# Second norm of a transformer-like step: broadcast ahead of three modulation units, a weight split on GpSimd

## The chip, the cores and the metric

One core of one Trainium2 chip. The metric is the device time of one execution in microseconds, median over runs. The engines are TensorE (PE: matmuls, PEld: its weight loads), VectorE (DVE), ScalarE (ACT), GpSimd (POOL) and SyncE (SP, which issues most DMAs).

## The reference

Two layers over 128 context tokens and 512 latent tokens, D = 1024, all float32. What matters here is the second norm and the MLP behind it, and the modulation vectors:

```python
m = (jax.nn.silu(cvec) @ w_mod[l] + b_mod[l])[..., None, :]
sh1, sc1, g1, sh2, sc2, g2 = jnp.split(m, N_MOD, axis=-1)
...
x = x + g1 * (jnp.concatenate([o, y], axis=-1) @ w_out[l])
h2 = _rmsnorm(x, norm2_g[l]) * (1 + sc2) + sh2
a, b = jnp.split(_dwconv3(h2 @ w_up[l], ffn_conv_w[l]), 2, axis=-1)
x = x + g2 * ((jax.nn.silu(a) * b) @ w_down[l])
```

## The kernel before, in words

Activations lie transposed: features on the 128 partitions, eight tiles k of them, and T = 644 columns for all tokens (both sequences with zero columns between), in two halves of 322. Each float32 product is made of three matmuls on rounded parts: a value v is split into hi = round(v) and lo = v - hi, and hi*hi, hi*lo and lo*hi are summed in PSUM.

Weights come in units of 128x2048 into two slots of `raw`, n = 0 to 17 in each layer; unit n uses slot n % 2. SP loads a unit, ACT makes `w_hi` (`split_hi`, L1238), DVE makes `w_lo` = raw - w_hi (`split_lo`, L1675), and PE uses both and frees the slot (`unit_done`). The order on every engine is written out by hand, and semaphores tie the engines together. Units 12 to 15 are the output projection. Units 16 (`G_U`) and 17 (`G_U + 1`) are w_up columns of the two "plain" gates, 0 and 6, computed directly; the other 20 gates go through a Strassen-like scheme of seven products, for which SP loads blocks (L518) and GpSimd issues DMAs that add one block to another (L621).

Around the second norm ("the gap") the program has this order:

- PE: the output projection's last chain; `mod_turn` (four 128x128 transposes of `mod_row`, L714); `stat` (one-column matmuls that sum x squared, L726); two modulation units on `mod_t` (`mod_sum`, L703, 8 small matmuls each; the trace counts every float32 matmul twice); `spread` (ones times a diagonal matrix, which puts 1/rms of every token on all partitions, L735); two modulation units on `mod_x`; `mod_turn`; then gate 0 in eight tiles k (`gate_tile`, L1049 to L1051), each after `h2_ready`, with another `mod_turn` behind tile 4; then gate 1, which waits for `split_full[1]`.
- ACT: `square` of each tile of x (L1393); the square root (`rms`, L1227); `rows`, a copy of the modulation sums out of PSUM (L1193), which waits for both `mod_t` units; `split_hi` of unit 17; then for each tile `h_full` (gain and shift, two instructions, L1411) and `h_high` (rounding to `hc_hi`, L1419), with another `rows` behind tile 2.
- DVE: the last addition to x; `reciprocals` (1/rms and the five 128x128 diagonals, L1666), which needs the square root; then for i = 0 to 9 the multiplication of x by the broadcast (L1976, for tile i) and the subtraction that gives `hc_lo` (L1984, for tile i - 2, after `h_high`). `mod_post` (L1621, L1624: adds the modulation parts) stands in turn i = 2 and `split_lo` of unit 17 in turn i = 5. After the loop the transformed inputs of the Strassen-like scheme are made.
- POOL: two loads and two stores early in the layer, then block sums only. SP: its first w_up block waits for `split_full[1]` of unit 17.

The modulation units of the gap are `GAP_A[l]` and the next: 10 and 11 in layer 0, 6 and 7 in layer 1. None of them is used by the second norm of its own layer.

Of the kernel before, what the change touches and what calls it, by code (L numbers as in the profile page):

```python
# [7 lines left out]
F32 = mybir.dt.float32  # L8
# [196 lines left out]
def hybrid_step(nc, x_prompt, x_sample, cache_k, cache_v, c_sample, c_ctx, w_mod, b_mod, norm1_g, w_in, q_norm_g,  # L205
# [3 lines left out]
    with ctx:  # L209
# [389 lines left out]
        @block.gpsimd  # L599
        def _(pool):  # L600
            ck = cache_k.rearrange("b l p h s d -> p (b l) (h s d)")
            cv = cache_v.rearrange("b l p h e -> p (b l) (h e)")
            nk = new_k.rearrange("b l p h s d -> p (b l) (h s d)")
            nv = new_v.rearrange("b l p h e -> p (b l) (h e)")
            for l in range(DEPTH):
                if l:
                    pool.wait_ge(stat_full, 3 * l + 1)
                else:
                    pool.wait_ge(rms_ready, 1)
                    pool.wait_ge(xT_read, 2 + KT)  # L610
                pool.dma_start(kc[:, :], ck[:, ds(l, 1), :].rearrange("p a n -> p (a n)")).then_inc(kv_in, 16)
                pool.wait_ge(mod_used, MOD_LAYER * l + MOD_PRE + 4)
                pool.dma_start(v[:, 1, :], cv[:, ds(l, 1), :].rearrange("p a n -> p (a n)")).then_inc(v_in, 16)
                pool.wait_ge(qk_ready, 2 * NT * l + NT + 1)
                pool.dma_start(nk[:, ds(l, 1), :].rearrange("p a n -> p (a n)"), qn[:, 0, :]).then_inc(nk_out, 16)
                pool.wait_ge(v_ready, NT * l + 1)
                pool.dma_start(nv[:, ds(l, 1), :].rearrange("p a n -> p (a n)"), v[:, 0, :]).then_inc(out_done, 16)

                def add_block(dst, src, which):

                    pool.dma_start(raw_f[:, BLK * dst:BLK * (dst + 1)], raw_f[:, BLK * src:BLK * (src + 1)],  # L621
                                   accum_op=ALU.add).then_inc(sum_full[which], 16)

                def first_sum(g):

                    a22, b = a22_block(g), s1_block(g)
                    pool.wait_ge(blk_full[a22], loaded(l, g, a22))
                    pool.wait_ge(blk_full[b], loaded(l, g, b))
                    add_block(b, a22, 1)

                first_sum(FIRST)
                for g in S_GATES:
                    pool.wait_ge(sum_full[1], summed(l, g))
                    pool.wait_ge(blk_full[2], loaded(l, g, 2))
                    add_block(2, s1_block(g), 2)
                    pool.wait_ge(blk_full[0], loaded(l, g, 0))
                    pool.wait_ge(blk_full[4], loaded(l, g, 4))
                    add_block(4, 0, 4)
                    pool.wait_ge(sum_full[2], summed(l, g))
                    pool.wait_ge(blk_full[5], loaded(l, g, 5))  # L640
                    add_block(5, 2, 5)
                    if g != S_GATES[-1]:
                        first_sum(S_GATES[S_GATES.index(g) + 1])
            pool.wait_ge(out_done, 16 * DEPTH)
            pool.wait_ge(nk_out, 16 * DEPTH)
# [17 lines left out]
        def _(pe):  # L663
# [12 lines left out]
            def mod_sum(l, h, u, b, landed_at):  # L676

                if b == "x" or b == "t":
                    pe.wait_ge(modx_full if b == "x" else modt_full, 32 * (l + 1))
                    wu = (mod_x if b == "x" else mod_t)[:, u, :].rearrange("p (t n) -> p t n", n=UC)  # L680
                    if b == "t" and u == 0:
                        pe.wait_ge(mod_ready, MOD_LAYER_G * l + h + MOD_PRE_G)
                elif b == "q":
                    pe.wait_ge(modq_full[2 * h + u], 16 * (l + 1))
                    wu = mod_q[:, 2 * h + u, :].rearrange("p (t n) -> p t n", n=UC)
                    if u == 0:
                        pe.wait_ge(mod_ready, MOD_LAYER_G * l + h + MOD_PRE_G)
                elif l is None:
                    if h == 1 and u == 0:
                        pe.wait_ge(mod_ready, 1)  # L690
                    elif h == 3 and u == 0:
                        pe.wait_ge(mod_ready, 3)
                    pe.wait_ge(pre_full[2 * h + u], 32)
                    wu = pre_unit(2 * h + u).rearrange("p (t n) -> p t n", n=UC)
                else:
                    pe.wait_ge(raw_full[b], landed_at)
                    wu = raw[:, b, :].rearrange("p (t n) -> p t n", n=UC)
                    if u == 0:
                        pe.wait_ge(mod_ready, MOD_LAYER_G * l + h + MOD_PRE_G)
                for part in range(2):  # L700
                    for q in range(4):
                        k = 4 * part + q
                        ins = mm(ps[QUAD * q:QUAD * (q + 1), mod_bank(l, h), u * UC:(u + 1) * UC], cT[:, k, :],  # L703
                                 wu[:, k, :], start=part == 0, stop=part == 1)
                ins.then_inc(mod_used, 1)
# [24 lines left out]
            def spread(l, which):  # L730

                for t, off, n, h, p0 in TILE_CUTS:
                    if off == 0:
                        pe.wait_ge(diag_ready, 3 * NT * l + (NT * which + t + 1))
                    ins = mm(ps[:, B_RMS[which][h], p0:p0 + n], ones[:, :], diag[:, t * P + off:t * P + off + n],  # L735
                             start=True, stop=True)
                    if off + n == P:
                        ins.then_inc(rb_full, 1)
# [47 lines left out]
            for l in range(DEPTH):  # L786
# [245 lines left out]
                    mod_turn(l, 9)  # L1032
                stat(l, 2)

                for u in range(2):
                    mod_sum(l, GAP_A[l], u, "t", None)
                spread(l, 2)
                for u in range(2):
                    mod_sum(l, GAP_A[l] + 1, u, "x", None)
                mod_turn(l, GAP_A[l])  # L1040
# [139 lines left out]
        def _(act):  # L1180
            A = nc.scalar.activation

            def rows(l, h):


                if l is None:
                    n = PRE_ORDER.index(h)
                    act.wait_ge(mod_used, 2 * n + 2)
                    if n:
                        act.wait_ge(modT_full, n)  # L1190
                else:
                    act.wait_ge(mod_used, MOD_LAYER * l + (MOD_PRE + 2 * h + 2))
                A(mod_row[:, :], ps[:, mod_bank(l, h), :], ACT.Copy).then_inc(row_read, 1)  # L1193
# [49 lines left out]
            for l in range(DEPTH):  # L1243
                def split_hi(n, i=None, size=SLOT):
                    split_hi_of(l, n, i, size)

                def rms(which, scale):
                    rms_of(l, which, scale)
# [147 lines left out]
                for n in range(4):  # L1396
                    square(2 * n)
                    if l < LAST:
                        rows(l, 6 + n)
                    square(2 * n + 1)  # L1400
                    if n < 3:
                        split_hi(O_U + n + 2)
                rms(2, 1.0 / D)
                rows(l, GAP_A[l])
                split_hi(G_U + 1)

                def h_full(k):

# [6 lines left out]
                def h_high(k):  # L1415

                    act.wait_ge(hf_ready, KT * l + k + 1)
                    base = k // KH * T
                    A(hb_hi[:, k % KH, base:base + T], hfull[:, k, :], ACT.Copy).then_inc(hh2_ready, 1)  # L1419

                h_full(0)
                h_high(0)
                h_full(1)
                for k in range(1, KT):
                    if k < KT - 1:
# [180 lines left out]
        def _(dve):  # L1606
# [91 lines left out]
            for l in range(DEPTH):  # L1698
# [275 lines left out]
                for i in range(KT + 2):  # L1974
                    if i < KT:
                        V.tensor_tensor(hfv[:, i, :, :], x[:, i, :].rearrange("p (h n) -> p h n", h=2),  # L1976
                                        ps[:, b0:b1 + 1, 0:HALF], ALU.mult).then_inc(xr_ready, 1)
                    if i == 2:
                        mod_post(l, GAP_A[l])
                    if i >= 2:  # L1980
                        k = i - 2
                        base = k // KH * T
                        dve.wait_ge(hh2_ready, KT * l + k + 1)
                        V.tensor_tensor(hb_lo[:, k % KH, base:base + T], hfull[:, k, :],  # L1984
                                        hb_hi[:, k % KH, base:base + T].bitcast(F32), ALU.subtract
                                        ).then_inc(h2_ready, 1)
                    if i == 5:
                        split_lo(G_U + 1)
                mod_post(l, GAP_A[l] + 1)

                h11, h12, h21, h22 = (hfv[:, KH * i:KH * (i + 1), h, :] for i in range(2) for h in range(2))
# [216 lines left out]
```

## Time and profile before

| | us |
|---|---|
| median of 3 runs | 1636.96 (1635.1 to 1638.65) |
| profiled execution, device time | 1639.15 |
| its span, first to last instruction | 1637.3 |
| PE busy in it | 1568.9 |
| DVE, ACT, POOL busy | 1032.3, 726.0, 142.7 |

In the timelines a row has the start in us from the span's start, the duration, engine, line, operation, what is written and read, the shapes, how many instructions the row merges and, in brackets, how long the engine stood idle before it and what released it. A row with xN covers N instructions from the first's start to the last's end.

### The profile page before, as it was taken

What the parts mean: (1) busy time and instruction counts of PE and PEld (TensorE: products, weight loads), DVE (VectorE), ACT (ScalarE), POOL (GpSimd) and SP (SyncE); (2) the same over time, 40 slices, a digit from 0 to 9 for tenths busy, and PEclk for the clock granted to TensorE, in tenths of its full rate; (3) what the DMA queues carried; (4) which work ended last, traced back from release to release, by engine and by line L of the source; (5) the groups of instructions that cost most, each with busy time, mean ns of one, the idle gap of its engine ahead of it and who ended that gap; (6) DMA issues with size and microseconds to landing.
All of it is one profiled execution on the core that took longest, in us unless ns stands there. A gap on an engine that the chain in (4) does not pass through costs nothing. (4 is left out here: it accounts for less than half of the span.)

```text
span 1637.3 us, 26294 instructions
## 1 busy us (share of the span) xinstructions
PE 1568.9 (96%) x10543; PEld 1460.5 (89%) x10543; DVE 1032.3 (63%) x1654; ACT 726.0 (44%) x1214; POOL 142.7 (9%) x172
## 2 busy tenths in 40 slices
PE   6999999988999999999979999999999999999998
PEld 4677888977999999999976788889899999999998
DVE  5752666645775765757776527667488667476573
ACT  3533444325662543525443344443366345163451
POOL 0000000000211201212000000000012011120210
PEclk9999999999999999999979999999999999999999
DMA  9555010473775956759631540115169476594862
GB/s 355 173 180 168 27 52 30 135 234 104 172 177 136 203 151 158 177 157 209 209 101 61 182 138 27 51 35 164 36 159 213 136 178 159 137 224 129 190 162 81
DMA packets 284043, 236.13 MB, mean 144 GB/s; under 512 B 10448, under 2 KB 254736, under 8 KB 283920
## 3 DMA queue, kind: packets, MB, share of 16 engines
q1 hardware_dynamic: 259392, 189.82, 37.0%
q0 software_dynamic: 23680, 44.05, 15.8%
q8 instruction: 84, 1.38, 0.4%
q10 hardware_dynamic: 848, 0.56, 0.1%
q14 instruction: 39, 0.32, 0.1%
HBM read 188.78 MB, written 3.67 MB: 118 GB/s over the span
## 5 line engine op out<-in xcount | busy, mean ns | idle before, releaser
L621 POOL DMA_DIRECT2D raw_all<-raw_all x160 | 137.9, 879 | 1130.5 <-DMA raw_all<-in_w_up_dram 996.1
L1512 ACT ACTIVATE w_hi<-raw_all 128x1024 fp32r<-128x1024 f32 x120 | 126.2, 1056 | 236.6 <-DMA raw_all<-raw_all 114.0
L1130 PE MATMUL ps<-gg,w_hi 128*128 128x322 f32 x704 | 219.2, 311 | 0.0
L1132 PE MATMUL ps<-gg,w_lo 128*128 128x322 f32 x704 | 218.7, 311 | 0.0
L2042 DVE TENSOR_TENSOR w_lo<-raw_all,w_hi 128x1024 fp32r<-128x1024 f32 x120 | 146.7, 1222 | 114.0 <-ACT w_hi L1512 113.3
L1131 PE MATMUL ps<-gg,w_hi 128*128 128x322 f32 x704 | 218.4, 310 | 0.0
L1075 PE MATMUL ps<-hc_lo,w_hi 128*128 128x322 f32 x640 | 199.6, 312 | 0.0
L1077 PE MATMUL ps<-hc_hi,w_lo 128*128 128x322 f32 x640 | 198.9, 311 | 0.0
L1073 PE MATMUL ps<-hc_hi,w_hi 128*128 128x322 f32 x640 | 198.7, 310 | 0.0
L1073 PE MATMUL ps<-ht_hi,w_hi 128*128 128x322 f32 x480 | 151.2, 315 | 5.7 <-ACT s L1530 3.6
L1077 PE MATMUL ps<-ht_hi,w_lo 128*128 128x322 f32 x480 | 149.0, 310 | 0.0
L1075 PE MATMUL ps<-ht_lo,w_hi 128*128 128x322 f32 x480 | 148.9, 310 | 0.0
L2003 DVE SCALAR_TENSOR_TENSOR tmp<-ub,vecs,tmp 128x642 f32<-128x642 f32 x168 | 139.5, 883 | 13.5 <-ACT tmp L1470 13.4
L1938 DVE SCALAR_TENSOR_TENSOR x<-ps,modv,x 128x128 f32<-128x128 f32 (+2 forms) x240 | 90.4, 434 | 90.6 <-PE ps L1132 53.7
L1675 DVE TENSOR_TENSOR w_lo<-raw_all,w_hi 128x2048 fp32r<-128x2048 f32 x36 | 82.4, 2289 | 95.3 <-ACT w_hi L1238 95.2
L1132 PEld LDWEIGHTS ps<-gg,w_lo 128*128 128x128 f32 x704 | 132.9, 189 | 0.0
L1131 PEld LDWEIGHTS ps<-gg,w_hi 128*128 128x128 f32 x704 | 132.8, 189 | 0.0
L1130 PEld LDWEIGHTS ps<-gg,w_hi 128*128 128x128 f32 x704 | 132.5, 188 | 0.1
L671 PE MATMUL ps<-h_hi,w_hi 128*128 128x322 f32 x384 | 122.7, 320 | 0.0
L1073 PEld LDWEIGHTS ps<-hc_hi,w_hi 128*128 128x128 f32 x640 | 120.8, 189 | 0.0
L1077 PEld LDWEIGHTS ps<-hc_hi,w_lo 128*128 128x128 f32 x640 | 120.6, 188 | 0.0
L1075 PEld LDWEIGHTS ps<-hc_lo,w_hi 128*128 128x128 f32 x640 | 120.4, 188 | 0.0
(206 smaller groups left out, 3455.8 us busy)
## 6 DMA issues: line engine op xcount, KB each, us to landing
raw_all<-in_w_up_dram SPq DMA_DIRECT2D x280, 256.0 KB, 3.8
raw_all<-raw_all POOLq DMA_DIRECT2D x160, 256.0 KB, 4.0
raw_all<-in_w_in_dram SPq DMA_DIRECT2D x48, 512.0 KB, 4.6
raw_all<-in_w_mod_dram SPq DMA_DIRECT2D x48, 512.0 KB, 4.4
raw_all<-in_w_down_dram SPq DMA_DIRECT2D x16, 768.0 KB, 4.4
raw_all<-in_w_down_dram SPq DMA_DIRECT2D x16, 640.0 KB, 4.2
mod_q<-in_w_mod_dram SPq DMA_DIRECT2D x8, 1024.0 KB, 11.2
raw_all<-in_w_out_dram SPq DMA_DIRECT2D x16, 512.0 KB, 4.4
```

The source lines that it names most:

```text
L621: pool.dma_start(raw_f[:, BLK * dst:BLK * (dst + 1)], raw_f[:, BLK * src:BLK * (src + 1)], accum_op=ALU.add).then_inc(sum_full[which], 16)
L671: mm(out, wh[:, k, col:col + P], mov_hi(k), start=k == 0, stop=False)
L1073: mm(out, whi_f[:, c0:c0 + P], hh[:, k, slot, :], start=first and k == 0, stop=False, skip_group_check=not first)
L1075: mm(out, whi_f[:, c0:c0 + P], hl[:, k, slot, :], start=False, stop=False, skip_group_check=not first)
L1077: ins = mm(out, wlo_f[:, c0:c0 + P], hh[:, k, slot, :], start=False, stop=k == KH - 1, skip_group_check=not first)
L1130: mm(out, wh[:, k, :], gh, start=k == 0, stop=False)
L1131: mm(out, wh[:, k, :], gl, start=False, stop=False)
L1132: ins = mm(out, wl[:, k, :], gh, start=False, stop=k == kf - 1)
L1512: A(whi_b[:, 2 * i:2 * (i + 1), :], src, ACT.Copy).then_inc(up_hi[i], 1)
L1938: ins = V.scalar_tensor_tensor(out=xs, in0=ps[:, banks[h], p0:p0 + n], scalar=gate, in1=xs, op0=ALU.mult, op1=ALU.add)
L2003: return V.scalar_tensor_tensor(out=cen[:, s, 1:T - 1], in0=u[:, s, j:j + T - 2], scalar=vecs[:, l, w:w + 1], in1=cen[:, s, 1:T - 1], op0= ...
L2042: V.tensor_tensor(wlo_b[:, pair, :], raw_b[:, pair, :] if i else first_pair(g), whi_b[:, pair, :].bitcast(F32), ALU.subtract).then_inc(up_ ...
```

## The change

Four edits, in both layers. PE: the second `mod_t` unit comes after `spread`. ACT: `split_hi` of unit 17 comes right behind the last square, ahead of `rms`; the first `rows` comes behind `h_high(0)`. DVE: the first `mod_post` stands in turn i = 3, and `split_lo` of unit 17 is gone. POOL: it makes that low half, with a `tensor_tensor` of its own that waits for `hi_done[1]` and signals `split_full[1]`.

```diff
--- before.py
+++ after.py
@@ -628,6 +628,9 @@
                     pool.wait_ge(blk_full[b], loaded(l, g, b))
                     add_block(b, a22, 1)
 
+                pool.wait_ge(hi_done[1], l * SPLIT_SLOT + (G_U + 1) // 2 + 1)
+                nc.gpsimd.tensor_tensor(w_lo[:, 1, :], raw[:, 1, :], w_hi[:, 1, :].bitcast(F32), ALU.subtract
+                                        ).then_inc(split_full[1], 1)
                 first_sum(FIRST)
                 for g in S_GATES:
                     pool.wait_ge(sum_full[1], summed(l, g))
@@ -1032,9 +1035,9 @@
                     mod_turn(l, 9)
                 stat(l, 2)
 
-                for u in range(2):
-                    mod_sum(l, GAP_A[l], u, "t", None)
+                mod_sum(l, GAP_A[l], 0, "t", None)
                 spread(l, 2)
+                mod_sum(l, GAP_A[l], 1, "t", None)
                 for u in range(2):
                     mod_sum(l, GAP_A[l] + 1, u, "x", None)
                 mod_turn(l, GAP_A[l])
@@ -1400,9 +1403,8 @@
                     square(2 * n + 1)
                     if n < 3:
                         split_hi(O_U + n + 2)
+                split_hi(G_U + 1)
                 rms(2, 1.0 / D)
-                rows(l, GAP_A[l])
-                split_hi(G_U + 1)
 
                 def h_full(k):
 
@@ -1420,6 +1422,7 @@
 
                 h_full(0)
                 h_high(0)
+                rows(l, GAP_A[l])
                 h_full(1)
                 for k in range(1, KT):
                     if k < KT - 1:
@@ -1975,7 +1978,7 @@
                     if i < KT:
                         V.tensor_tensor(hfv[:, i, :, :], x[:, i, :].rearrange("p (h n) -> p h n", h=2),
                                         ps[:, b0:b1 + 1, 0:HALF], ALU.mult).then_inc(xr_ready, 1)
-                    if i == 2:
+                    if i == 3:
                         mod_post(l, GAP_A[l])
                     if i >= 2:
                         k = i - 2
@@ -1984,8 +1987,6 @@
                         V.tensor_tensor(hb_lo[:, k % KH, base:base + T], hfull[:, k, :],
                                         hb_hi[:, k % KH, base:base + T].bitcast(F32), ALU.subtract
                                         ).then_inc(h2_ready, 1)
-                    if i == 5:
-                        split_lo(G_U + 1)
                 mod_post(l, GAP_A[l] + 1)
 
                 h11, h12, h21, h22 = (hfv[:, KH * i:KH * (i + 1), h, :] for i in range(2) for h in range(2))
```

PE in layer 0, from the last transposes of the output projection to gate 0. Before:

```order
L726 MATMUL ps<-ones,sq 128x1 x5
L703 MATMUL ps<-mod_t,cT 32x256 x16
L735 MATMUL ps<-sq,ones 128x128 x2
L735 MATMUL ps<-sq,ones 128x64 x2
L735 MATMUL ps<-sq,ones 128x128 x2
L703 MATMUL ps<-mod_x,cT 32x256 x16
L714 MATMUL ps<-ident,mod_row 128x128 x4
L1049 MATMUL ps<-hc_hi,w_hi 128x322
```

With the change:

```order
L729 MATMUL ps<-ones,sq 128x1 x5
L706 MATMUL ps<-mod_t,cT 32x256 x8
L738 MATMUL ps<-sq,ones 128x128 x2
L738 MATMUL ps<-sq,ones 128x64 x2
L738 MATMUL ps<-sq,ones 128x128 x2
L706 MATMUL ps<-mod_t,cT 32x256 x8
L706 MATMUL ps<-mod_x,cT 32x256 x16
L717 MATMUL ps<-ident,mod_row 128x128 x4
L1052 MATMUL ps<-hc_hi,w_hi 128x322
```

Eight of the sixteen `mod_t` matmuls moved behind the six of `spread`.

ACT in layer 0, from the last square on (`w_hi` is unit 17's high half, `mod_row` the row copy, `hfull` the shift). Before:

```order
L1393 ACTIVATE sq<-x 128x644
L1227 ACTIVATE rms<-rms,eps 128x5
L1193 ACTIVATE mod_row<-ps 128x512
L1238 ACTIVATE w_hi<-raw_all 128x2048
L1411 ACTIVATE hfull<-hfull,modv,gain 128x128
L1411 ACTIVATE hfull<-hfull,modv,gain 128x512
L1419 ACTIVATE hc_hi<-hfull 128x644
L1411 ACTIVATE hfull<-hfull,modv,gain 128x128
L1411 ACTIVATE hfull<-hfull,modv,gain 128x512
L1411 ACTIVATE hfull<-hfull,modv,gain 128x128
```

With the change:

```order
L1396 ACTIVATE sq<-x 128x644
L1241 ACTIVATE w_hi<-raw_all 128x2048
L1230 ACTIVATE rms<-rms,eps 128x5
L1413 ACTIVATE hfull<-hfull,modv,gain 128x128
L1413 ACTIVATE hfull<-hfull,modv,gain 128x512
L1421 ACTIVATE hc_hi<-hfull 128x644
L1196 ACTIVATE mod_row<-ps 128x512
L1413 ACTIVATE hfull<-hfull,modv,gain 128x128
L1413 ACTIVATE hfull<-hfull,modv,gain 128x512
L1413 ACTIVATE hfull<-hfull,modv,gain 128x128
```

The high half moved ahead of the square root, and the row copy behind the first tile's `hc_hi`.

DVE in layer 0, from turn i = 4 of the loop on (`w_lo` is unit 17's low half). Before:

```order
L1976 TENSOR_TENSOR hfull<-x,ps 128x644
L1984 TENSOR_TENSOR hc_lo<-hfull,hc_hi 128x644
L1976 TENSOR_TENSOR hfull<-x,ps 128x644
L1984 TENSOR_TENSOR hc_lo<-hfull,hc_hi 128x644
L1675 TENSOR_TENSOR w_lo<-raw_all,w_hi 128x2048
L1976 TENSOR_TENSOR hfull<-x,ps 128x644
L1984 TENSOR_TENSOR hc_lo<-hfull,hc_hi 128x644
L1976 TENSOR_TENSOR hfull<-x,ps 128x644
L1984 TENSOR_TENSOR hc_lo<-hfull,hc_hi 128x644 x3
```

With the change, and below it GpSimd's queue where the work went:

```order
L1979 TENSOR_TENSOR hfull<-x,ps 128x644
L1987 TENSOR_TENSOR hc_lo<-hfull,hc_hi 128x644
L1979 TENSOR_TENSOR hfull<-x,ps 128x644
L1987 TENSOR_TENSOR hc_lo<-hfull,hc_hi 128x644
L1979 TENSOR_TENSOR hfull<-x,ps 128x644
L1987 TENSOR_TENSOR hc_lo<-hfull,hc_hi 128x644
L1979 TENSOR_TENSOR hfull<-x,ps 128x644
L1987 TENSOR_TENSOR hc_lo<-hfull,hc_hi 128x644 x3
```

```order
L615 DMA out_dram<-qn 128x512
L617 DMA out_dram<-v 128x512
L632 ISA
L632 TENSOR_TENSOR w_lo<-raw_all,w_hi 128x2048
L621 DMA raw_all<-raw_all 128x512 x80
```

The subtraction of 128x2048 left DVE and stands on GpSimd between the layer's last store and its first block sum, with an ISA instruction ahead of it in layer 0 (none in layer 1).

## Rows read from the trace of the kernel before

**Rows 1.** First part of the page: busy us, share, instructions of each engine.
```profile
PE 1568.9 (96%) x10543; PEld 1460.5 (89%) x10543; DVE 1032.3 (63%) x1654; ACT 726.0 (44%) x1214; POOL 142.7 (9%) x172
```
**Rows 2.** Waits of PE over the span: total us, times, longest.
```profile
PE ps L1049 <- DVE hc_lo L1984: 7.5, 6, 1.6
```
**Rows 3.** Timeline of PE in layer 1's gap.
```profile
1175.51 1.93 PE L703 MATMUL ps<-mod_t,cT 128*32 128x256 f32 x32
1177.38 1.60 PE L735 MATMUL ps<-sq,ones 128*128 128x128 f32 x12
...
1182.86 0.39 PE L1049 MATMUL ps<-hc_hi,w_hi 128*128 128x322 f32 x1 [1.43 <-DVE hc_lo L1984]
...
1189.50 0.42 PE L1049 MATMUL ps<-hc_hi,w_hi 128*128 128x322 f32 x1
...
1193.18 0.41 PE L1049 MATMUL ps<-hc_hi,w_hi 128*128 128x322 f32 x1 [1.63 <-DVE hc_lo L1984]
```
**Rows 4.** Timeline of ACT in layer 1's gap.
```profile
1173.51 0.74 ACT L1393 ACTIVATE sq<-x 128x644 f32<-128x644 f32 x1 [6.38 <-DVE x L1938]
1175.82 0.30 ACT L1227 ACTIVATE rms<-rms,eps 128x5 f32<-128x5 f32 x1 [1.57 <-DVE rms L1660]
1177.51 0.60 ACT L1193 ACTIVATE mod_row<-ps 128x512 f32<-128x512 f32 x1 [1.39 <-PE ps L703]
1178.01 1.90 ACT L1238 ACTIVATE w_hi<-raw_all 128x2048 fp32r<-128x2048 f32 x1
...
1181.76 2.28 ACT L1411 ACTIVATE hfull<-hfull,modv,gain 128x128 f32<-128x128 f32 x4
1183.94 0.72 ACT L1419 ACTIVATE hc_hi<-hfull 128x644 fp32r<-128x644 f32 x1
...
1185.66 0.72 ACT L1419 ACTIVATE hc_hi<-hfull 128x644 fp32r<-128x644 f32 x1
...
1187.86 0.72 ACT L1419 ACTIVATE hc_hi<-hfull 128x644 fp32r<-128x644 f32 x1
...
1192.42 1.20 ACT L1411 ACTIVATE hfull<-hfull,modv,gain 128x128 f32<-128x128 f32 x2 [2.11 <-DVE hfull L1976]
```
**Rows 5.** Timeline of DVE in layer 1's gap and after it.
```profile
1176.42 1.07 DVE L1666 TENSOR_SCALAR sq<-ident,rms 128x128 f32<-128x128 f32 x5
1179.02 2.29 DVE L1976 TENSOR_TENSOR hfull<-x,ps 128x644 f32<-128x644 f32 x3 [1.52 <-PE ps L735]
...
1184.69 0.83 DVE L1984 TENSOR_TENSOR hc_lo<-hfull,hc_hi 128x644 fp32r<-128x644 f32 x1 [1.25 <-ACT hc_hi L1419]
...
1189.37 2.28 DVE L1675 TENSOR_TENSOR w_lo<-raw_all,w_hi 128x2048 fp32r<-128x2048 f32 x1
...
1217.65 1.22 DVE L2042 TENSOR_TENSOR w_lo<-raw_all,w_hi 128x1024 fp32r<-128x1024 f32 x1 [3.89 <-ACT w_hi L1512]
```
**Rows 6.** Stretches: us, then busy us of PE, PEld, DVE, ACT, POOL; PEclk; DMA.
```profile
380.00:384.00 4.00, 4.00 (x35) 1.81 (x35) 1.44 (x7) 0.66 (x2) 0.00 (x0) 0.50 0.00 0
1200.90:1215.40 14.50, 14.50 (x99) 14.50 (x98) 12.64 (x11) 7.20 (x9) 4.32 (x5) 1.00 0.74 165
```
**Rows 7.** Timeline of PE, ACT and DVE in layer 0's gap.
```profile
378.02 1.99 PE L726 MATMUL ps<-ones,sq 128*128 128x1 f32 x10 [0.55 <-ACT sq L1393]
379.94 3.64 PE L703 MATMUL ps<-mod_t,cT 128*32 128x256 f32 x32
380.25 0.30 ACT L1227 ACTIVATE rms<-rms,eps 128x5 f32<-128x5 f32 x1 [2.28 <-DVE rms L1660]
383.50 2.41 PE L735 MATMUL ps<-sq,ones 128*128 128x128 f32 x12
385.96 2.30 DVE L1976 TENSOR_TENSOR hfull<-x,ps 128x644 f32<-128x644 f32 x3 [4.04 <-PE ps L735]
388.70 2.28 ACT L1411 ACTIVATE hfull<-hfull,modv,gain 128x128 f32<-128x128 f32 x4
```
**Rows 8.** Groups by line of POOL: busy us, mean ns of one.
```profile
L2196 POOL MEMSET const-float32-0.0<- 128x1 f32 x1 | 0.1, 98 | 0.2 <-issue 0.2
```
**Rows 9.** Timeline of SP's DMA queue in layer 1's gap.
```profile
1191.68 38.61 SPq L518 DMA_DIRECT2D raw_all<-in_w_up_dram  x20
```

## The prediction

> **What bounds the kernel now.** I read the profile's first part, then the waits of the tensor engine (PE), then the timelines of PE, ScalarE (ACT) and VectorE (DVE) through the gap between output projection and first plain gate, in both layers, and last the clock and the DMA queue there. PE is busy 96% of the span and ends last [rows 1]: an edit pays only if it shortens PE's own idle time or its slow stretches. One of PE's largest waits is the first plain gate waiting for hc_lo, 7.5 us in 6 waits over two layers [rows 2]. The change works just there.
>
> The timeline of layer 1 shows the gap at full clock [rows 3]: two mod_t units run from 1175.51 for 1.93 us, then the broadcast (`spread`, L735) for 1.60, then two mod_x units and the transposes, and gate 0 starts at 1182.86. But DVE had begun the diagonals for the broadcast at 1176.42 and finished at 1177.49 [rows 5]: the second mod_t unit kept it waiting. After that the work is a chain for each of 8 tiles k: DVE multiplies x by the broadcast (0.82 us), ACT shifts it (two instructions, 1.2 us) and rounds it to hc_hi (0.74), DVE subtracts to hc_lo (0.83), PE computes tile k of gate 0. Starts overlap the previous instruction's end by some 0.1 us, so ACT needs 1.72 us per tile (1183.94 to 1185.66), and 2.2 us where it also copies a row of modulation (1185.66 to 1187.86) [rows 4]. PE needs 1.8 us per tile, since gate 1, eight like tiles, takes 14.5 us unbroken [rows 6]. ACT and PE are thus nearly level, and any delay in the chain reaches PE. One is large: DVE's 2.28 us split_lo at 1189.37 makes ACT wait 2.11 us for its next tile, and PE 1.63 us before tile 4 [rows 3, 4, 5].
>
> Layer 0 has the same gap with one difference: the granted clock stands at 0.50, the 1.2 GHz level, over 380 to 384. The mod_t units take 3.64 us instead of 1.93, the broadcast 2.41 instead of 1.60 [rows 3, 6, 7].
>
> **The broadcast earlier.** In layer 1 the first mod_t unit, half of 1.93, ends at 1176.5. ACT now makes the high half right behind the last square: it starts as the square ends, about 1174.2, and lasts 1.90, to 1176.1, so the rms square root, at 1175.82 before, slips by 0.2 us [rows 4], and the diagonals end at 1177.7. The broadcast follows them one by one, and its last tile lands about 0.5 us behind the last diagonal, at 1178.2, where before it ended at 1178.98. DVE's first multiply starts **0.8 us earlier**. In layer 0 the square root waits for the statistics anyway (380.25); the square there ends at about 377.9, as PE's matmuls on it start at 378.02, so the high half is done at about 379.8, in time; first unit 379.94 to 381.8, broadcast 2.4 at the low clock, to 384.25: DVE starts **1.7 us earlier** than 385.96 [rows 7].
>
> **The row copy behind the first tile.** `rows`, 0.6 us, stood with the high half before the first shift, both hidden by the wait for the broadcast. It now stands between h_high(0) and h_full(1), on the chain, and costs its 0.5 to 0.6 there. So h_full(1) moves by 0.8 - 0.5 = 0.3 us in layer 1 (1181.76 to 1181.45) and by 1.7 - 0.5, about 1.25, in layer 0 (388.70 to 387.45) [rows 4, 7]. The transposes wait for this copy: PE stands idle about 0.6 us in front of them, and gate 0 starts at 1182.0, 0.85 earlier, but tile 1 only 0.3 earlier. The moved modulation sum on DVE (0.36 us) falls into a wait of 1.25 for hc_hi and costs nothing. The modulation unit moved past the broadcast costs nothing: the same instructions, needed by nothing before the row copy.
>
> **split_lo off DVE.** ACT's wait of 2.11 us vanishes. Late next is PE itself: tile 3 starts at 1189.50, so tile 4 could at 1191.3 and starts at 1193.18 [rows 3]; **1.9 us per layer** go. Nothing takes its place, since the remaining chain goes at 1.72 us against PE's 1.8.
>
> **The subtraction on GpSimd.** No trace row shows GpSimd doing arithmetic on a tile. From below the nearest row is DVE's same instruction, 2.28 us [rows 5]; GpSimd's own nearest is a 128x1 memset of 98 ns [rows 8], a fixed cost only. From above I can bound it only by its cover: gate 1 needs it at 404.6 in layer 0 and 1198.6 in layer 1 (new times), and the high half is ready at 379.8 and 1176.1. Anything up to 22.5 us costs nothing; I take it so, because the row on DVE is ten times shorter than that cover. The GPSIMD Engine Reference of the Trainium skill (Performance versus the Vector engine) gives 4.5 us for a 2048-element fp32 tensor_tensor, twice VectorE's; the sum would be the same by it. Behind this wait on GpSimd's queue stands only the first block sum of the layer, whose blocks are loaded after the subtraction in any case. The DMA queue waits for the same semaphore before its w_up blocks: it starts them some 10 us earlier than 1191.68 [rows 9], with nothing else to move; no gain, as ACT's first up-split also needs gate 0's end.
>
> **The sum.** Layer 1: 1.9 + 0.3 = 2.2. Layer 0: 1.9 + 1.25 = 3.15. Together 5.3 us off a span of 1637.3, leaving 1632.0. Behind gate 0 stand 14.5 us of gate 1, in which DVE runs out of work and then idles 3.89 us for the next high half [rows 5], and its work has moved forward as far as PE's; later phases are PE's, so the gain is kept. The profiled execution took 1639.15, 2.2 above the median of 1636.96, and the clock step of layer 0 may be missing in other runs: then layer 0 gains what layer 1 does. I forecast 1636.96 - 5.2 = **1631.8 us**. A measurement of this kernel tells about 0.2%, 3.3 us, from no change, so faster means below 1633.7.
>
> **Rivals.**
> *Port.* DVE runs slower beside GpSimd. At stake are the instructions between high half and end of the subtraction: diagonals 1.07 and three multiplies 2.29 [rows 5]. If they all took twice as long: 3.4 us a layer at worst, 6.7 in all, and the gain is gone; half of that, a size between nothing and the worst, gives about 1635. Against it: two of the three ends are guesses, and in layer 0 the multiplies start 4.4 us after the high half. The GPSIMD Engine Reference (Key points) says that GpSimd shares its SBUF interfaces with VectorE and collides with instructions in a 2-port mode or with two SBUF inputs. By that rule the multiplies, with one input in PSUM, would be spared. No row of this trace can decide it.
> *Clock.* The low level seen at 380 to 384 came right after sparse one-column matmuls and a 0.55 us wait [rows 6, 7]. The new order adds a wait before the broadcast and one before the transposes. If layer 1 falls to 0.5 as well, the first mod_t unit takes 0.9 longer and the broadcast 0.8, and with the latency behind it some 2 us are given back: about 1634.
> *GpSimd late.* If its subtraction ends after gate 0, PE waits for it, and the change is slower. It decides from 22.5 us (layer 1) and 24.6 (layer 0); break-even over both is about 26. At 30 us gate 1 would start at 409.8 and 1206.1 instead of 407.7 and 1200.9, 2.1 + 5.2 = 7.3 us later than before: 1644. For it: nothing shows GpSimd's speed, and the new order has an extra ISA instruction ahead of the first subtraction, whose price no row shows. Against it: ten times DVE's time.
> *Nothing carried.* The gaps close but another wait in front of gate 1 or the up phase, such as the transformed inputs on DVE, takes the time: 1637. Against it: gate 1 runs unbroken, and DVE's work ends before it does [rows 5, 6].
>
> **Chances.** Forecast 0.66; port 0.13, clock 0.10, late GpSimd 0.05, nothing carried 0.06. The forecast's own spread is 1629.5 to 1634 (the scatter of runs, 1635.1 to 1638.65, and the clock step present or not); port and clock reach to 1635.5. I give 1629.0 to 1635.6. Faster: nearly all of the forecast and a third of clock, 0.68. Same: the rest of these and nothing carried, 0.25. Slower: late GpSimd and the worst of port, 0.07.
>
> **What would show it.** Right: no PE wait before tile 4; PE's wait for hc_lo at about 3 us instead of 7.5; the broadcast starting within 0.4 us of the first diagonal; the subtraction on GpSimd over before 390 and 1190; the DMA queue's first block there too. Wrong: a wait of PE for GpSimd at gate 1; diagonals or multiplies longer than 0.28 and 0.82; a PE clock under 1.0 in layer 1's gap; PE idle in the first up products.

## The result, and the profile after

The change made the kernel **slower**: 1639.77 us median (20 runs) against 1636.34 for the kernel before (20 runs), ratio 1.0028 with a 95% interval of 1.0019 to 1.0037. (The two medians alone would give 1.0021, which the interval contains.) I had forecast 1631.8 and a range of 1629.0 to 1635.6. The profiled execution has a span of 1640.2 us, 2.9 above the one of before.

Waits of PE in the changed kernel (total us, times, longest):

```profile
PE ps L738 <- DVE sq L1669: 8.2, 3, 4.0
...
PE ps L1052 <- DVE hc_lo L1987: 1.7, 2, 1.1
```

The wait that the change was to shorten did shrink, from 7.5 us [rows 2] to 1.7. A new one of 8.2 us stands in its place: `spread` (now L738) waits for the diagonals (L1669). Timeline of layer 1's gap, PE and POOL, to be held against [rows 3]:

```profile
1175.41 1.28 PE L706 MATMUL ps<-mod_t,cT 128*32 128x256 f32 x16
1180.66 2.93 PE L738 MATMUL ps<-sq,ones 128*128 128x128 f32 x12 [3.98 <-DVE sq L1669]
1183.52 1.94 PE L706 MATMUL ps<-mod_t,cT 128*32 128x256 f32 x16
...
1190.68 0.41 PE L1052 MATMUL ps<-hc_hi,w_hi 128*128 128x322 f32 x1 [0.61 <-DVE hc_lo L1987]
```
```profile
1176.03 4.49 POOL L632 TENSOR_TENSOR w_lo<-raw_all,w_hi 128x2048 fp32r<-128x2048 f32 x1 [224.77 <-ACT w_hi L1241]
```

and DVE in the same stretch, against [rows 5]:

```profile
1176.17 0.19 DVE L1666 RECIPROCAL rms<-rms 128x5 f32<-128x5 f32 x1 [0.49 <-ACT rms L1230]
1176.44 4.95 DVE L1669 TENSOR_SCALAR sq<-ident,rms 128x128 f32<-128x128 f32 x5
1183.63 2.30 DVE L1979 TENSOR_TENSOR hfull<-x,ps 128x644 f32<-128x644 f32 x3 [2.24 <-PE ps L738]
```

The five diagonals take 4.95 us instead of 1.07. The view of that one line (min, median, max of its five instructions, ns) shows how it is shared out:

```profile
L1669 DVE TENSOR_SCALAR sq<-ident,rms x5: 274/274/4169, 1176.4 to 1181.1; 128x128 f32<-128x128 f32 x5
```

One instruction takes 4.17 us, the other four 0.27 each. The long one began at 1176.44 and so ended at about 1180.6; GpSimd's subtraction ended at 1176.03 + 4.49 = 1180.52. DVE did not go slower: it **stood still until GpSimd was done**. PE stood still with it. The granted clock was at the 1.2 GHz level through that wait and the broadcast behind it. The stretch 1174 to 1186 in the kernel before, then in the changed one (columns as in [rows 6]):

```profile
1174.00:1186.00 12.00, 9.58 (x105) 7.12 (x106) 6.94 (x16) 9.01 (x15) 0.00 (x0) 1.00 0.01 2
```
```profile
1174.00:1186.00 12.00, 7.82 (x62) 5.43 (x66) 7.61 (x10) 3.62 (x6) 4.54 (x2) 0.59 0.36 104
```

The mean granted clock there is 0.59 instead of 1.00, and the broadcast takes 2.93 us instead of 1.60. The wait didn't bring the clock down, though. Two short stretches of the changed kernel show the fall while PE was still busy with the first `mod_t` unit, before the wait began at about 1176.7:

```profile
1175.00:1176.00 1.00, 1.00 (x17) 0.81 (x20) 0.17 (x1) 1.00 (x2) 0.00 (x0) 1.00 0.00 0
1176.00:1176.50 0.50, 0.50 (x12) 0.00 (x0) 0.25 (x2) 0.14 (x1) 0.47 (x1) 0.63 0.00 0
```

So two things are mixed here, the hold and the clock. The experiments take them apart.

A measure for all that follows is the **gap length**: from the first `stat` matmul to the first matmul of the first Strassen-like product. Both ends are rows of the PE timeline. Before: 376.30 to 422.05 and 1172.14 to 1215.11, so 45.75 us in layer 0 (low clock in part) and 42.97 in layer 1 (full clock). With the change: 378.22 to 424.10 and 1172.04 to 1218.31, so 45.88 and 46.27. Together 3.4 us more, where the spans differ by 2.9. Outside the gaps the profiled executions scatter by a few us (e7 below has gaps 7.0 us shorter than the kernel before, and a span 12.2 us shorter), so for the gap I go by gap lengths, and for the time of a kernel by the ratios.

### The profile page after: what moved, and what is told of

It is laid out like the page before. It is cut to its first block and busy times, and to the rows that moved or that the text cites. A ratio compares the mean times of both kernels' runs of the same rounds, so it can differ in the third digit from the quotient of the medians.

```text
span 1640.2 us, 26296 instructions
## 1 busy us (share of the span) xinstructions
PE 1571.1 (96%) x10543; PEld 1463.8 (89%) x10543; DVE 1036.7 (63%) x1652; ACT 725.8 (44%) x1214; POOL 150.4 (9%) x174
## 5 line engine op out<-in xcount | busy, mean ns | idle before, releaser
L1678 DVE TENSOR_TENSOR w_lo<-raw_all,w_hi 128x2048 fp32r<-128x2048 f32 x34 | 77.8, 2289 | 96.6 <-ACT w_hi L1241 96.5
```

## The experiments

Ratios are to the kernel before, run on the same chip, five rounds each.

| run | ratio (95%) | gap, layer 0 / 1, us |
|---|---|---|
| the change | 1.0028 (1.0019 to 1.0037) | 45.88 / 46.27 |
| e1 GpSimd behind the diagonals | 0.9977 (0.9961 to 0.9992) | 42.91 / 42.44 |
| e2 low half back on DVE | 1.0009 (0.9998 to 1.0021) | 44.86 / 44.29 |
| e3 before, low half on GpSimd | 1.0012 (1.0001 to 1.0024) | 44.65 / 44.94 |
| e4 diagonals with two inputs | 1.0035 (1.0023 to 1.0047) | 45.95 / 46.35 |
| e5 diagonals on ACT | 0.9994 (0.9981 to 1.0008) | 41.96 / 43.84 |
| e6 e1, old order on PE | 0.9988 (0.9976 to 0.9999) | 40.66 / 42.67 |
| e7 e1 with dense fillers | 0.9961 (0.9947 to 0.9975) | 40.65 / 41.09 |
| e8 GpSimd behind the first hc_hi | 1.0017 (1.0002 to 1.0032) | 44.95 / 43.84 |
| e9 before with dense fillers | 0.9997 (0.9985 to 1.0009) | 43.18 / 43.60 |
| e10 the change with dense fillers | 1.0018 (1.0005 to 1.0031) | 45.88 / 46.28 |
| e11 e1 with sparse fillers | 0.9975 (0.9962 to 0.9987) | 41.93 / 42.28 |
| e12 e5 with dense fillers | 0.9965 (0.9952 to 0.9978) | 40.88 / 42.59 |

### Is it GpSimd, or the new order? (e1, e2)

e1 is the change with one wait more on GpSimd:

```diff
                 pool.wait_ge(hi_done[1], l * SPLIT_SLOT + (G_U + 1) // 2 + 1)
+                pool.wait_ge(diag_ready, 3 * NT * l + 3 * NT)
```

> GpSimd's subtraction waits for the five diagonals as well, all else as in the change. Theory A (only VectorE's tensor_scalar on the SBUF tile, the diagonals, is held by GpSimd's tensor_tensor; multiplies with one operand in PSUM are not): diagonals 1.1 us again, three multiplies 2.3 us, the time comes out where I forecast the change, 5 us below the kernel before (ratio 0.997). Theory B (any VectorE instruction that reads SBUF is held): the three multiplies take 5 to 6 us and hc_lo(0) is late, time 2 to 6 us above the kernel before. Theory C (the new order on TensorE and ScalarE costs, not GpSimd): time stays 3 to 5 us above the kernel before.

Timeline of e1, layer 1, DVE, then POOL:

```profile
1173.10 1.07 DVE L1670 TENSOR_SCALAR sq<-ident,rms 128x128 f32<-128x128 f32 x5
1176.41 2.29 DVE L1980 TENSOR_TENSOR hfull<-x,ps 128x644 f32<-128x644 f32 x3 [2.24 <-PE ps L739]
```
```profile
1174.32 4.56 POOL L633 TENSOR_TENSOR w_lo<-raw_all,w_hi 128x2048 fp32r<-128x2048 f32 x1 [227.92 <-DVE sq L1670]
```

One wait turns 1.0028 into 0.9977. The diagonals are back at 1.07 us, and the three multiplies, one operand of each in PSUM, run inside GpSimd's 4.56 us at 2.29, untouched. Theory A holds, B falls, and C falls as the explanation of the change's time. The gain of 3.7 us is short of the 5 expected. Per layer the hold had cost 45.88 - 42.91 = 3.0 and 46.27 - 42.44 = 3.8 us of gap in these profiles.

e2 removes the subtraction from GpSimd and puts `split_lo(G_U + 1)` back into turn i = 5.

> The change with the low half back on VectorE in turn 5 and nothing on GpSimd: the reordering alone. Theories A and B: by the terms of the prediction 0.3 us in layer 1 and 1.25 in layer 0 are won, 1.5 us below the kernel before, ratio 0.999. Theory C: 3 to 5 us above it.

The PE wait before tile 4 is back, at the size of [rows 3] (timeline of PE, layer 1):

```profile
1189.69 0.41 PE L1049 MATMUL ps<-hc_hi,w_hi 128*128 128x322 f32 x1 [1.63 <-DVE hc_lo L1984]
```

The reordering alone won nothing: 1.0009, where I had expected 0.999 (and where theory C would have had at least 1.002). Against e1, which differs in the place of the low half alone, the gaps are 1.95 and 1.85 us longer: the term of 1.9 us per layer for `split_lo` was right.

### Which instructions are held? (e3, e4, e5, e8)

e3 is the kernel before with only the low half moved, where ACT makes the high half after the row copy, as before.

> The kernel before with one edit: the low half on GpSimd instead of VectorE, where ScalarE makes the high half late (ready about 1179.9 in layer 1). Diagonals are over by then. Theory A: the multiplies are untouched, PE's wait before tile 4 is gone, 1.9 us per layer, 3.8 us below the kernel before (0.9977), unless hc_lo(0), with two SBUF inputs, is held until the subtraction ends near 1184.4: then tile 0 starts 2.5 us late per layer and little is won. Theory B: multiplies 5 us, slower by 2 us or more.

DVE and POOL in layer 1:

```profile
1177.64 2.29 DVE L1979 TENSOR_TENSOR hfull<-x,ps 128x644 f32<-128x644 f32 x3 [3.15 <-PE ps L738]
1180.09 0.19 DVE L1624 TENSOR_REDUCE modv<-ps 128x8 f32<-128x32 f32 x1 [0.15 <-PE ps L717]
1180.35 2.39 DVE L1627 TENSOR_TENSOR modv<-modv,vecs 128x8 f32<-128x8 f32 x1
```
```profile
1178.16 4.55 POOL L632 TENSOR_TENSOR w_lo<-raw_all,w_hi 128x2048 fp32r<-128x2048 f32 x1 [229.80 <-ACT w_hi L1241]
```

The smallest instruction in the loop pays. In the kernel before, this addition of 8 columns, with both inputs in SBUF, was

```profile
1181.74 0.17 DVE L1624 TENSOR_TENSOR modv<-modv,vecs 128x8 f32<-128x8 f32 x1
```

Now it takes 2.39 us and ends at 1182.74, GpSimd at 1182.71. hc_lo(0) queues behind it, so tile 0 is late, though it was not itself the first to be held. That is theory A in a wider form: instructions with two SBUF inputs are held too. The ratio is 1.0012, and not the 0.9977 that I had expected if nothing were held.

e4 writes the diagonals as identity x 1/rms x identity:

```diff
-                    V.tensor_scalar(diag[:, t * P:(t + 1) * P], ident[:, :], rms5[:, t:t + 1], None, ALU.mult
-                                    ).then_inc(diag_ready, 1)
+                    V.scalar_tensor_tensor(out=diag[:, t * P:(t + 1) * P], in0=ident[:, :], scalar=rms5[:, t:t + 1],
+                                           in1=ident[:, :], op0=ALU.mult, op1=ALU.mult).then_inc(diag_ready, 1)
```

> The change with the diagonals made by scalar_tensor_tensor (identity times 1/rms times identity: two SBUF inputs, same values) instead of tensor_scalar, GpSimd early as in the change. If only the one-input tensor_scalar form is held (Theory A, narrow): diagonals about 1.1 us, time 5 us below the kernel before. If two SBUF inputs are held too (A, wide): diagonals near 4.9 us and the time as the change's, 3 to 5 us above. A result between, diagonals of 1.5 to 3 us, would say that the engines share instead of one waiting for the other.

```profile
L1669 DVE SCALAR_TENSOR_TENSOR sq<-ident,rms x5: 338/340/4236, 1176.4 to 1181.3; 128x128 f32<-128x128 f32 x5
```

Held just the same: two SBUF inputs, first instruction 4.24 us. The unheld four also take 0.340 us where tensor_scalar took 0.274. Additions and subtractions with two SBUF inputs take 0.17 us for 8 columns and 0.83 for 644, so about 1.04 ns a column, or 133 ns for 128. An estimate from these rows: 66 ns less for 128 columns is what a tensor_scalar would save that moves its columns at twice the speed. The Trainium skill (Advanced Engine Details and Errata, Mode Summary) says that VectorE moves two elements a cycle in a mode that has source and destination in SBUF and uses two read ports, that the second of these ports is shared with GpSimd, and that the two "will interfere/block eachother". That agrees with the diagonals: 4169 ns against 274.

e5 makes the second norm's diagonals on ACT (copy of the identity with scale 1/rms, behind a semaphore that DVE raises after the reciprocal), GpSimd early as in the change.

> The change with GpSimd as early as in it, but the five diagonals of the second norm made by ScalarE (copy of the identity scaled by 1/rms). If the hold is between GpSimd's tensor_tensor and VectorE's SBUF-only instructions, ScalarE is free of it: diagonals of some 0.25 us each, broadcast not held, multiplies from PSUM 2.3 us as in the first experiment, time near that one (3.8 us below the kernel before), minus half a microsecond per layer for the hand-over. If the SBUF itself were short, ScalarE's diagonals would be long as well (over 3 us) and the time above the kernel before. VectorE's reciprocal (128x5) stands just behind GpSimd's start and may be held: then its start or end slips by up to 4.5 us and this run is as slow as the change.

ACT, DVE and POOL of e5 in layer 1:

```profile
1170.97 1.57 ACT L1411 ACTIVATE sq<-ident,rms 128x128 f32<-128x128 f32 x5 [0.29 <-DVEq L1672]
```
```profile
1170.72 0.19 DVE L1671 RECIPROCAL rms<-rms 128x5 f32<-128x5 f32 x1 [0.37 <-ACT rms L1231]
1174.83 2.29 DVE L1987 TENSOR_TENSOR hfull<-x,ps 128x644 f32<-128x644 f32 x3 [3.92 <-PE ps L739]
```
```profile
1169.68 4.52 POOL L633 TENSOR_TENSOR w_lo<-raw_all,w_hi 128x2048 fp32r<-128x2048 f32 x1 [226.32 <-ACT w_hi L1242]
```

ACT writes the same tile beside GpSimd in 0.3 us apiece: SBUF as such isn't short. The reciprocal, one SBUF input, isn't held either. The ratio, 0.9994, is that of the kernel before, where I had expected some 3 us less. Its interval overlaps e1's; the low clock cost this run too (layer 1, 43.84), and what else it lost I can't say.

e8 lets GpSimd start only after the first `hc_hi` (a wait for `hh2_ready`).

> The change with GpSimd's subtraction waiting for the first hc_hi, so that it runs beside hc_lo(0), multiply 3, the modulation sum and hc_lo(1). If VectorE instructions with all operands in SBUF are held until GpSimd ends (as the modulation sum was at 2.39 us in the third experiment), hc_lo(0) or the next such instruction ends only with GpSimd, TensorE's first tiles start 3 to 4 us late per layer, and the time is 1 to 4 us above the kernel before. If 644-column instructions that have started keep their turn, hc_lo(0) takes 0.83 us and only the next one is held. If two-input ones share, each takes up to twice its time and little is lost.

```profile
1180.13 0.83 DVE L1988 TENSOR_TENSOR hc_lo<-hfull,hc_hi 128x644 fp32r<-128x644 f32 x1 [0.57 <-ACT hc_hi L1422]
1180.88 0.82 DVE L1980 TENSOR_TENSOR hfull<-x,ps 128x644 f32<-128x644 f32 x1
1181.62 0.18 DVE L1625 TENSOR_REDUCE modv<-ps 128x8 f32<-128x32 f32 x1
1181.87 3.54 DVE L1628 TENSOR_TENSOR modv<-modv,vecs 128x8 f32<-128x8 f32 x1
```
```profile
1180.25 5.14 POOL L633 TENSOR_TENSOR w_lo<-raw_all,w_hi 128x2048 fp32r<-128x2048 f32 x1 [231.31 <-ACT hc_hi L1422]
```

Both directions in one picture. hc_lo(0), begun 0.12 us ahead of GpSimd, keeps its 0.83, and GpSimd takes 5.14 instead of 4.5. The next instruction with two SBUF inputs waits 3.5 us, to 1185.41, GpSimd's end being 1185.39; a multiply and a reduction from PSUM between them pass free. **Of two instructions that exclude each other, the one that has begun runs to its end, and the other waits for it**: VectorE's 0.83 us there, GpSimd's 5.14 here.

### And the clock? (e6, e7, e9 to e12)

e6 is e1 with TensorE's order of before, and `rows` again ahead of the first shift.

> The first experiment (GpSimd behind the diagonals, ScalarE's high half early) with TensorE's order of before (both mod_t units ahead of the broadcast) and the row copy hidden in front of the first shift again. By the terms of the prediction: 1.9 us per layer from split_lo, nothing from the broadcast: 3.8 us below the kernel before. If the new TensorE order costs through the clock (it was at 0.50 in all four profiled gaps of the first and second experiments, in one of two in the kernel before), this is as fast as the first experiment or faster, 4 to 6 us below. hc_lo(0), two SBUF inputs, falls beside GpSimd's last half microsecond: if such instructions are held it ends with GpSimd.

Layer 0, at full clock, has a gap of 40.66 us, 2.3 below the full-clock gap of before (layer 1's, 42.97); layer 1 shows 42.67 with its broadcast at 2.64 us. The ratios of e6 and e1 overlap. In layer 1 hc_lo(0) came 1.2 us after GpSimd's end. In layer 0 it began 0.4 us ahead of that end (385.53) and took 1.11 us instead of 0.83:

```profile
385.11 1.11 DVE L1988 TENSOR_TENSOR hc_lo<-hfull,hc_hi 128x644 fp32r<-128x644 f32 x1 [0.57 <-ACT hc_hi L1423]
```

Low clock in these gaps is frequent. In the six profiled gaps with the old TensorE order and no fillers (before, e3, e6) the broadcast took 1.6 us in three and 2.0 to 2.6 in three. In the fourteen with the new order and no dense fillers (change, e1, e2, e4, e5, e8, e11) it took 2.4 to 2.9 in all fourteen. The hold is not the reason, as e1, e2, e5, e8 and e11 have no held diagonals. e7 adds work that is thrown away to e1, in bank 5, which nothing uses there:

```diff
+            def filler(l, n):
+
+                pe.wait_ge(split_full[0], usable(l, G_U))
+                for k in range(n):
+                    mm(ps[:, 5, 0:HALF], w_hi[:, 0, k * P:(k + 1) * P], h_hi[:, k, 0:HALF], start=True, stop=True)
...
+                    if last and which == 2:
+                        filler(l, 4)
...
                 mod_sum(l, GAP_A[l], 0, "t", None)
+                filler(l, 2)
                 spread(l, 2)
```

> The first experiment plus throw-away 128x322 matmuls into an unused PSUM bank, four in TensorE's wait for the last square and two behind the first mod_t unit, per layer. If the low clock in the gap follows from TensorE's own sparse work there, the granted clock stays at 1.00 in both layers more often, the broadcast takes 1.6 instead of 2.9 us, and the time is 2 to 4 us below the first experiment. If the clock falls whatever runs there, the fillers cost their own 0.3 us beside nothing and the time is that of the first experiment or up to 1 us above.

Layer 1 of e7, PE, then DVE, then the stretch from the second `stat` part to the row copy:

```profile
1165.05 1.07 PE L707 MATMUL ps<-mod_t,cT 128*32 128x256 f32 x16
1166.45 1.58 PE L747 MATMUL ps<-sq,ones 128*128 128x128 f32 x12
1167.96 1.07 PE L707 MATMUL ps<-mod_t,cT 128*32 128x256 f32 x16
```
```profile
1168.07 2.29 DVE L1989 TENSOR_TENSOR hfull<-x,ps 128x644 f32<-128x644 f32 x3 [0.92 <-PE ps L747]
1170.93 1.62 DVE L1997 TENSOR_TENSOR hc_lo<-hfull,hc_hi 128x644 fp32r<-128x644 f32 x1 [0.57 <-ACT hc_hi L1431]
```
```profile
1163.80:1170.80 7.00, 6.91 (x88) 4.78 (x88) 3.73 (x10) 3.82 (x5) 3.50 (x1) 1.00 0.01 4
```

Clock 1.00, broadcast 1.58, gaps of 40.65 and 41.09 us, and the lowest ratio of all: **0.9961, 6.3 us below** the kernel before (medians 1630.46 and 1636.77). Its interval overlaps that of e1, so the traces show what the fillers do to the clock, and the times don't yet show a gain from them. hc_lo(0) is held here for 0.8 us, as GpSimd ends at 1171.85.

e9 is the kernel before with the same six fillers, e10 the change with them.

> The kernel before plus the same six throw-away matmuls per layer (four in the wait for the last square, two between the mod_t units): the clock lever without the change. If the gap's clock falls cost the kernel before as well (one of its two profiled gaps stood at 0.50), the clock stays at 1.00 in both and the time is 1 to 3 us below the kernel before, gap of layer 0 near 43 instead of 45.8 us. If the fillers help only the new order, the time is that of the kernel before, plus 0 to 0.6 us for the two fillers that hide behind no wait.

> The change, GpSimd early, plus the same fillers: the hold with the clock kept as far as fillers can. The hold stays, diagonals 4.8 us. The gap should be longer than the 41.1 us of the filler run by the hold, 3.7 us, if the clock survives TensorE's wait of 4 us, and by 5 us or more if it falls in that wait: 45 to 46 us, and 1 to 4 us above the kernel before.

e9 kept the full clock in both gaps (43.18 and 43.60 us) and is no faster: 0.9997, where I had thought 1 to 3 us possible. The fillers don't make a kernel fast by themselves. They also cost something there: e9's layer 1 gap is 0.6 us longer than that of the kernel before (42.97), both at full clock. At full clock the repaired order gives 40.65 and 41.09 against 43.18 and 43.60, so **2.5 us per layer** against e9, and **1.9 us** in layer 1 against the kernel before without fillers.

That gain is not shown to come from the broadcast's new place. e6 has the old order on TensorE and no fillers, and its full-clock layer 0 gap is 40.66, e7's 40.65.

e10 still holds the diagonals (4.96 us). PE in layer 1, then two stretches:

```profile
1170.51 1.07 PE L706 MATMUL ps<-mod_t,cT 128*32 128x256 f32 x16
1171.51 0.56 PE L725 MATMUL ps<-h_hi,w_hi 128*128 128x322 f32 x2
1175.78 2.93 PE L746 MATMUL ps<-sq,ones 128*128 128x128 f32 x12 [3.71 <-DVE sq L1678]
```
```profile
1171.00:1174.50 3.50, 1.07 (x14) 0.39 (x6) 3.15 (x2) 0.24 (x2) 3.37 (x1) 1.00 0.00 0
1175.00:1180.00 5.00, 4.22 (x28) 3.31 (x32) 2.76 (x7) 0.40 (x1) 0.81 (x2) 0.50 0.60 174
```

PE waits 3.71 us, the clock falls in that wait, and the gaps are 45.88 and 46.28: 5.2 us above e7 in each layer. e10 and e7 differ in the one wait on GpSimd alone, and their intervals lie apart. So 5.2 us is the hold's full price where the clock is not already low, the clock lost in PE's wait included.

e11 replaces 322 columns by 16, with 8 and 4 fillers.

> The first experiment with fillers of 16 columns instead of 322, twice as many (8 and 4): TensorE is as unidle as in the filler run but does a tenth of the work. If dense work is what keeps the clock, it falls as in the first experiment: 0.50 in the gap, broadcast 2.9 us, time that of the first experiment (ratio 0.998). If not standing idle is enough, clock 1.00, broadcast 1.6 us, ratio 0.996.

```profile
1169.60:1178.20 8.60, 8.57 (x90) 6.04 (x90) 4.04 (x11) 4.22 (x6) 4.55 (x1) 0.80 0.01 3
```

PE is busy for 8.57 of 8.60 us and the clock still falls (0.80 on average, broadcast 2.71); the ratio is e1's, and its interval overlaps e7's too. So standing idle is not what lowers the clock here. What differs from e7, where it stayed up, is that the fillers are 16 columns wide and not 322, and twice as many. The profiled gaps were 41.93 and 42.28.

> Diagonals on ScalarE, GpSimd early, plus the fillers: no VectorE instruction with SBUF-only operands falls beside GpSimd but possibly none, as GpSimd is over before hc_lo(0). Against the filler run hc_lo(0) is not held (1.62 to 0.83 us), tile 0 starts up to 0.7 us earlier, but the diagonals come about 0.5 us later. Gap 40.5 to 41.5 us per layer, ratio 0.995 to 0.997; a tie with the filler run is the likeliest.

e12 has no held DVE instruction at all, and ties with e7 (0.9965), as expected. Its layer 0 gap, at full clock, is 40.88 where e7 has 40.65; its layer 1 lost the clock in spite of the fillers (broadcast 2.29, gap 42.59). Six fillers are thus no guarantee.

## Why the prediction was wrong, step by step

- **The step that failed is the subtraction on GpSimd, costed at nothing.** I looked for its cover and found 22.5 us, and it was over after 4.5. But I asked only who waits for it, and not whom it makes wait. It runs beside the diagonals, on the critical path, and holds them to its end: 3.0 and 3.8 us per layer (change against e1), 5.2 in each where the clock was up before it (e10 against e7).
- **The rival "port" named the mechanism and missed its size and its victims.** I priced it as instructions taking twice as long, spread over diagonals and multiplies. It is a lock: 0.27 us became 4.17 for one instruction, and the multiplies, which I counted as the larger share, were spared in every run in which they ran beside GpSimd (2.29 or 2.30 us for three in e1, e3, e5, e6, e7, e11 and e12). The rule of the Trainium skill (GPSIMD Engine Reference, Key points) that I cited names two kinds of instruction, those in a 2-port mode and those with two SBUF inputs; I applied it to the multiplies and didn't ask it about the diagonals. With "held until GpSimd ends" the sum was at hand: GpSimd from 1176.1 for its 4.5 us, diagonals done at 1181.6 instead of 1177.7, the gap 3.9 us longer than forecast in layer 1.
- **The rival "clock" also came true**, in every profiled gap of the new order without dense fillers. In layer 1 of e1 it makes the broadcast 1.33 us longer, and the gap is 42.44, where my terms gave 42.97 - 2.2 = 40.8 at full clock. The repaired order won 3.7 us (ratio 0.9977, medians 1633.55 and 1637.25) and not 5.3; the broadcast's 1.33 us are most of the difference, if the profiled gap is typical, which isn't shown.
- **The term of `split_lo` stood**: 1.9 us per layer forecast, 1.95 and 1.85 measured (e2 against e1). PE's wait before tile 4 is gone in the change too; its wait for hc_lo fell to 1.7 us, and I had said about 3. GpSimd's 4.49 us agree with the 4497 ns of the Trainium skill (GPSIMD Engine Reference, Performance versus the Vector engine). SP's first w_up block went from 1191.68 [rows 9] to 1180.55, and no gain from it shows. At full clock the whole repaired order gains 1.9 us in layer 1 (e7 against before) or 2.5 per layer (e7 against e9), against a forecast of 2.2.
- **The term of the broadcast is not confirmed.** The row copy behind tile 0 and the earlier broadcast together were to win 0.3 and 1.25 us. e2 has them alone and is not faster, and e6, without either, has as short a gap at full clock as e7. In layer 0 its gap is 44.86 against 45.75 (0.9 less, both at low clock in part); in layer 1 it is 44.29 against 42.97 at full clock, where it lost the clock.

Two slips in the prediction changed nothing: rounding to hc_hi takes 0.72 us [rows 4] and not 0.74, and the cover in layer 0 is 404.6 - 379.8 = 24.8 us and not 24.6.

What stays open: what the earlier broadcast is worth at full clock; whether fillers pay beyond the noise; and how often each order loses the clock over many runs. The trace shows one execution of each kernel. The mean granted clock over all runs points the same way (0.988 before, 0.983 for the change, 0.986 for e1, 0.989 for e7), but doesn't say where in the span it was lost. Why ScalarE's diagonals in e5 came out no faster than the kernel before is open as well.

## What to carry to other kernels

Before moving elementwise work to GpSimd, list what VectorE has to do in that window, and look for pieces with two inputs in SBUF and for tensor_scalar from SBUF to SBUF: beside GpSimd's tensor_tensor each of these waited for it to end, even one of 8 columns. Work with an input in PSUM, and the same work on ScalarE, went free. Start the GpSimd instruction behind the short critical VectorE ones (a single wait was worth half a per cent here). And look at TensorE's granted clock before pricing a stretch of one-column and small matmuls: in 17 of the 20 profiled gaps without dense fillers the broadcast ran partly or wholly at the low level.

## What the runs showed of the hardware that I had not expected

- GpSimd's tensor_tensor and VectorE exclude each other for whole instructions: 4169 ns instead of 274 (tensor_scalar, one SBUF input), 4236 instead of 340 (scalar_tensor_tensor), 2.39 and 3.54 us instead of 0.17 (8-column addition), 1.62 instead of 0.83 (hc_lo). In the other direction GpSimd took 5.14 us instead of 4.5 (e8). A reciprocal of 128x5 in SBUF, reductions from PSUM and multiplies with one PSUM operand kept their times.
- TensorE's clock fell to 0.50 while the engine was busy 8.57 of 8.60 us with one-column, 16-column and small modulation matmuls. In five of six gaps it stayed at full through the broadcast when six matmuls of 322 columns stood among them (e7, e9, e12). In both gaps of e10, with the same six, it fell in the 3.7 us wait.
